# Reordering the column tiles of an input projection: attention-gate tiles between the GLU pairs, four V tiles around the LayerNorm

## What is computed

```python
p_x = h_x @ w_in[i]                      # 1024 x 8192
q_x = apply_rope(rms(p_x[..., Q0:K0]), cos, sin)
k_x = apply_rope(rms(p_x[..., K0:V0]), cos, sin)
v_x = p_x[..., V0:GA0]
att_x  = diff_attn_branch(q_x, k_all, v_all, ...)     # context and latent keys
a, g = jnp.split(p_x[..., U0:GC0], 2, axis=-1)
y = depthwise_conv(a * jax.nn.sigmoid(g), conv_w, conv_b)   # 31 taps
conv_x = silu(layernorm(y, ln_g, ln_b))               # over the 1024 channels
mixed_x = concatenate([att_x  * silu(p_x[..., GA0:U0]),
                       conv_x * silu(p_x[..., GC0:IN_W])])
y_x = mixed_x @ w_out[i]
```

## Time and profile before

| | |
|---|---|
| median of 3 runs | 2513.55 us (2512.09 to 2514.61) |
| span of the profiled execution, first to last instruction | 2509.4 us |
| own time of the profiled execution | not listed apart; the median is 4.15 us over its span |
| mean granted TensorE clock | 0.974 |
| PE busy | 2317.3 us, 92% of the span |
| DVE / POOL / ACT busy | 1323.7 / 875.1 / 849.3 us |
| taps of the convolution (L999) | 365.2 us, 240 instructions |
| ACT table loads | 9 of 1.28 us in the whole kernel |

### The profile page before, as it was taken

How to read it: one execution, slowest core, us unless ns; L and a number is a source line. 1 busy time by engine, 2 the same in 40 slices (tenths; PEclk the granted TensorE clock), 3 DMA queues, 4 the chain that set the end, 5 groups by cost and what they waited for, 6 DMA issues and landing times. The chain is left out here.

```text
span 2509.4 us, 30851 instructions
## 1 busy us (share of the span) xinstructions
PE 2317.3 (92%) x10898; PEld 1846.8 (74%) x10898; DVE 1323.7 (53%) x1373; ACT 849.3 (34%) x1244; POOL 875.1 (35%) x600
## 2 busy tenths in 40 slices
PE   4799999999968999999999999968888888899998
PEld 2445888888746788887787788857777777788787
DVE  5754339999992200016556540079999995800101
ACT  5745511111101212222222211157777774222221
POOL 0004823333311222221221222136656653844443
PEclk9999999999989999999999999989999997999999
DMA  8977621111111122221221232332221105153433
GB/s 290 337 247 219 193 66 46 50 46 46 46 42 51 55 72 71 67 72 54 72 75 53 72 97 72 87 89 57 59 59 48 48 1 206 67 176 127 160 129 108
DMA packets 227184, 246.46 MB, mean 98 GB/s; under 512 B 11277, under 2 KB 163853, under 8 KB 225583
## 3 DMA queue, kind: packets, MB, share of 16 engines
q1 hardware_dynamic: 225680, 235.11, 29.8%
q0 software_dynamic: 1440, 10.49, 1.1%
HBM read 214.09 MB, written 31.47 MB: 98 GB/s over the span
## 5 line engine op out<-in xcount | busy, mean ns | idle before, releaser
L448 POOL TENSOR_TENSOR w_lo<-w_raw,w_hi 128x512 fp32r<-128x512 f32 x288 | 402.7, 1409 | 1067.3 <-ACT w_hi L700 1066.9
L570 PE MATMUL psum<-h_hi,w_hi 128*128 128x512 f32 x1792 | 561.6, 395 | 6.5 <-POOL w_lo L448 4.9
L570 PE MATMUL psum<-h_hi,w_lo 128*128 128x512 f32 x1792 | 552.8, 390 | 0.0
L570 PE MATMUL psum<-h_lo,w_hi 128*128 128x512 f32 x1792 | 552.6, 390 | 0.0
L700 ACT ACTIVATE w_hi<-w_raw 128x512 fp32r<-128x512 f32 x288 | 180.8, 631 | 1036.9 <-PE psum L570 729.6
L570 PEld LDWEIGHTS psum<-h_hi,w_hi 128*128 128x128 f32 x1792 | 337.3, 188 | 85.3 <-issue 16.5
L570 PEld LDWEIGHTS psum<-h_lo,w_hi 128*128 128x128 f32 x1792 | 337.1, 188 | 70.6
L570 PEld LDWEIGHTS psum<-h_hi,w_lo 128*128 128x128 f32 x1792 | 336.9, 188 | 70.3
L999 DVE SCALAR_TENSOR_TENSOR conv<-y_pad,tap_w,conv 128x1024 f32<-128x1024 f32 x240 | 365.2, 1522 | 9.4
L1675 POOL TENSOR_TENSOR wo_lo<-wo_raw,wo_hi 128x512 fp32r<-128x512 f32 x128 | 175.8, 1380 | 188.4 <-ACT wo_hi L1758 188.4
L84 PE MATMUL psum<-wo_hi,m_hi 128*128 128x512 f32 x512 | 202.0, 395 | 10.7 <-DVE m_lo L1791 6.5
(11 more groups left out here) (174 smaller groups left out, 3182.8 us busy)
## 6 DMA issues: line engine op xcount, KB each, us to landing
w_raw<-in_w_in_dram SPq DMA_DIRECT2D x288, 256.0 KB, 3.0
ada_w<-in_w_ada_dram SPq DMA_DIRECT2D x32, 1024.0 KB, 6.8
wo_raw<-in_w_out_dram SPq DMA_DIRECT2D x128, 256.0 KB, 3.0
proj<-stage SPq DMA_DIRECT2D x40, 512.0 KB, 3.1
gate_w<-in_w_ada_dram SPq DMA_DIRECT2D x16, 1024.0 KB, 5.0
x_tok<-in_x_dram POOLq DMA_DIRECT2D x8, 1024.0 KB, 7.2
k_raw<-proj SPq DMA_DIRECT2D x16, 512.0 KB, 5.7
q_raw<-proj SPq DMA_DIRECT2D x16, 512.0 KB, 6.2
```

The costliest lines, as they stand in the source:

```text
L448: pool.tensor_tensor(w_lo[:, c], w_raw[:, c], w_hi[:, c].bitcast(F32), ALU.subtract).then_inc(w_lo_ready[c], 1)
L570: mm = pe.matmul(bank(2 * s_ + hf), w[:, c, j, :], x[:, jj, hf * BANK:(hf + 1) * BANK], start=(jj == 0 and w is w_hi and x is h_hi), stop= ...
```

## The change

The tiles of the projection are computed in another order. New numbers: U and GA in triples 16 to 39 (value, gate, GA tile), V 0 to 3 at 40 to 43, GC 44 to 51, K 52 to 59, Q 60 to 67, V 4 to 7 at 68 to 71. The rows of `proj` in DRAM stay where they were, now by `ROW_*` constants. PE takes the mean sums after V 0 and V 1, the sums of squares after V 2, then V 3. On ACT, two tiles (V 0, V 1) stand before the squares and V 2 right after them, with a load of the Sqrt table ahead of it; the split of V 3's weights is in `to_stage` of V 2. GA tiles take the parity of their number, so U tiles now use either pair of banks. Waits and counts of stores follow. Nothing is added to or left out of the computation.

```diff
@@ -50,7 +50,9 @@
 
 
 
-N_VC, N_KC, N_U, N_GA, N_GC, N_K, N_Q, N_V, N_END = 0, 8, 16, 32, 40, 48, 56, 64, 72
+N_VC, N_KC, N_U, N_V0, N_GC, N_K, N_Q, N_V4, N_END = 0, 8, 16, 40, 44, 52, 60, 68, 72
+
+ROW_GA, ROW_GC, ROW_K, ROW_Q, ROW_V, ROW_END = 0, 8, 16, 24, 32, 40
 
...
@@ -385,41 +387,70 @@
                 for s_ in range(2):
...
+            load_w(N_U, U0)
+            store_ctx(N_U - 3, 1, ctx_normed, CT - 2)
+            load_w(N_U + 1, U0 + CONV_W)
+            store_ctx(N_U - 2, 0, ctx_normed, CT - 1)
+            store_ctx(N_U - 1, 1, ctx_normed, CT)
+            load_w(N_U + 2, GA0)
+            load_w(N_U + 3, U0 + P)
+            load_w(N_U + 4, U0 + CONV_W + P)
+            store_after_act(N_U + 2, ROW_GA, 0)
+            load_w(N_U + 5, GA0 + P)
+
+            with sp.Fori(1, CT // 2) as i:
+                for s_ in range(2):
+                    n = N_U + 6 * i + 3 * s_
+                    load_w(n, U0 + (2 * i + s_) * P)
+                    load_w(n + 1, U0 + CONV_W + (2 * i + s_) * P)
+                    store_after_act(n - 1, ROW_GA + 2 * i + s_ - 1, 1 - s_)
+                    load_w(n + 2, GA0 + (2 * i + s_) * P)
+
+            load_w(N_V0, V0)
+            load_w(N_V0 + 1, V0 + P)
+            store_after_act(N_V0 - 1, ROW_GA + CT - 1, 1)
+            for k in range(2, 4):
+                load_w(N_V0 + k, V0 + k * P)
+                store_after_act(N_V0 + k - 2, ROW_V + k - 2, k % 2)
+            for k in range(2):
+                load_w(N_GC + k, GC0 + k * P)
+                store_after_act(N_GC + k - 2, ROW_V + k + 2, k)
+            with sp.Fori(1, CT // 2) as i:
+                for s_ in range(2):
+                    load_w(N_GC + 2 * i + s_, GC0 + (2 * i + s_) * P)
...
             for s_ in range(2):
-                load_w(N_U + s_, U0 + s_ * CONV_W)
-                store_ctx(N_U + s_ - 3, 1 - s_, ctx_normed, CT + s_ - 2)
-            store_ctx(N_U - 1, 1, ctx_normed, CT)
-            with sp.Fori(1, CT) as i:
-                for s_ in range(2):
-                    load_w(N_U + 2 * i + s_, U0 + i * P + s_ * CONV_W)
-            for n0, col0, last_store, own_store in ((N_GA, GA0, None, store_after_act),
-                                                    (N_GC, GC0, store_after_act, store_gc),
-                                                    (N_K, K0, store_gc, store_qk),
-                                                    (N_Q, Q0, store_qk, store_qk),
-                                                    (N_V, V0, store_qk, store_after_act)):
-                for s_ in range(2):
-                    load_w(n0 + s_, col0 + s_ * P)
-                    if last_store:
-                        last_store(n0 + s_ - 2, s_)
-                if n0 == N_K:
-
-                    sp.wait_ge(conv_used, CT)
-                    sp.dma_start(cos[:], t["rope_cos"]).then_inc(rope_landed, 16)
-                    sp.dma_start(sin[:], t["rope_sin"]).then_inc(rope_landed, 16)
+                load_w(N_K + s_, K0 + s_ * P)
+                store_gc(CT + s_ - 2, s_)
+
+            sp.wait_ge(conv_used, CT)
+            sp.dma_start(cos[:], t["rope_cos"]).then_inc(rope_landed, 16)
+            sp.dma_start(sin[:], t["rope_sin"]).then_inc(rope_landed, 16)
+            for n0, col0, k0 in ((N_K, K0, 0), (N_Q, Q0, CT)):
+                if k0:
+                    for s_ in range(2):
+                        load_w(n0 + s_, col0 + s_ * P)
+                        store_qk(k0 + s_ - 2, s_)
                 with sp.Fori(1, CT // 2) as i:
                     for s_ in range(2):
                         load_w(n0 + 2 * i + s_, col0 + (2 * i + s_) * P)
-                        own_store(n0 + 2 * i + s_ - 2, s_)
+                        store_qk(k0 + 2 * i + s_ - 2, s_)
+            for k in range(2):
+                load_w(N_V4 + k, V0 + (4 + k) * P)
+                store_qk(2 * CT + k - 2, k)
+            for k in range(2, 4):
+                load_w(N_V4 + k, V0 + (4 + k) * P)
+                store_after_act(N_V4 + k - 2, ROW_V + 4 + k - 2, k % 2)
...
@@ -583,9 +614,13 @@
                     pe.wait_ge(psum_freed, n + s_ - N_U - 1)
                     tile(n + s_, s_)
 
-            with pe.Fori(1, CT) as i:
-                pair(N_U + 2 * i)
-            pair(N_GA)
+            for n in range(N_U + 2, N_U + 6):
+                pe.wait_ge(psum_freed, n - N_U - 1)
+                tile(n, n % 2)
+            with pe.Fori(1, CT // 2) as i:
+                for q in range(3):
+                    pair(N_U + 6 * i + 2 * q)
+            pair(N_V0)
 
             pe.wait_ge(ctx_root, CT)
             for i in range(CT):
@@ -594,15 +629,16 @@
                     mm = pe.matmul(bank(4 + hf), mean_ones[:], conv[:, i, hf * BANK:(hf + 1) * BANK],
                                    start=(i == 0), stop=(i == CT - 1))
             mm.then_inc(mean_done, 1)
-            pair(N_GA + 2)
+            pe.wait_ge(psum_freed, N_V0 + 2 - N_U - 1)
+            tile(N_V0 + 2, 0)
             for i in range(CT):
                 pe.wait_ge(ln_squared, i + 1)
                 for hf in range(2):
                     mm = pe.matmul(bank(6 + hf), mean_ones[:], evac[:, i % 2, hf * BANK:(hf + 1) * BANK],
                                    start=(i == 0), stop=(i == CT - 1))
                 mm.then_inc(ln_sq_used, 1)
-            with pe.Fori(2, 4) as i:
-                pair(N_GA + 2 * i)
+            pe.wait_ge(psum_freed, N_V0 + 3 - N_U - 1)
+            tile(N_V0 + 3, 1)
             with pe.Fori(0, 4) as i:
                 pair(N_GC + 2 * i)
 
@@ -622,14 +658,13 @@
                     tile(n, s_)
                     pe.wait_ge(qk_root, 2 * i + s_ - 1)
                     qk_sums(2 * i + s_ - 1, (s_ + 1) % 2)
-            pe.wait_ge(psum_freed, N_V - N_U - 1)
-            tile(N_V, 0)
+            pe.wait_ge(psum_freed, N_V4 - N_U - 1)
+            tile(N_V4, 0)
             pe.wait_ge(qk_root, 2 * CT - 1)
             qk_sums(2 * CT - 1, 1)
-            pe.wait_ge(psum_freed, N_V - N_U)
-            tile(N_V + 1, 1)
-            with pe.Fori(1, 4) as i:
-                pair(N_V + 2 * i)
+            pe.wait_ge(psum_freed, N_V4 - N_U)
+            tile(N_V4 + 1, 1)
+            pair(N_V4 + 2)
 
         @block.scalar
...
@@ -751,18 +786,24 @@
                     ctx_square(k, s_)
                     ctx_sqrt(k - 1, (s_ + 1) % 2)
 
-            def glu_value(n, i, first=False):
+            def glu_value(n, i, s_):
                 split_w(n + 1)
                 act.wait_ge(tile_done, n + 1)
-                if not first:
-                    act.wait_ge(glu_used, i)
-                nc.scalar.activation(evac[:, 0, :], bank(0, 2), ACT.Copy).then_inc(psum_freed, 1)
-
-            def glu_gate(n):
+                act.wait_ge(glu_used, i)
+                nc.scalar.activation(evac[:, 0, :], bank(2 * s_, 2), ACT.Copy).then_inc(psum_freed, 1)
+
+            def glu_gate(n, s_):
...
@@ -770,33 +811,31 @@
             act.preload_act_table(ACT.Sigmoid)
             act.wait_ge(tile_done, N_U + 1)
             nc.scalar.activation(evac[:, 0, :], bank(0, 2), ACT.Copy).then_inc(psum_freed, 1)
-            glu_gate(N_U + 1)
-            with act.Fori(1, CT) as i:
-                glu_value(N_U + 2 * i, i)
-                glu_gate(N_U + 2 * i + 1)
-
-            def to_stage(n, s_, count, func, last=False):
-
-                if not last:
-                    split_w(n + 1)
-                act.wait_ge(tile_done, n + 1)
-                act.wait_ge(stored[s_], count)
-                nc.scalar.activation(stage[:, s_, :], bank(2 * s_, 2), func).then_inc(psum_freed, 1)
-
-            act.preload_act_table(ACT.Silu)
-            for k in range(4):
-                to_stage(N_GA + k, k % 2, 16 * (CT + k // 2), ACT.Silu)
+            glu_gate(N_U + 1, 1)
+            to_stage(N_U + 2, 0, 16 * CT, ACT.Silu)
+            glu_value(N_U + 3, 1, 1)
+            glu_gate(N_U + 4, 0)
+            to_stage(N_U + 5, 1, 16 * CT, ACT.Silu)
+            with act.Fori(1, CT // 2) as i:
+                for s_ in range(2):
+                    n = N_U + 6 * i + 3 * s_
+                    glu_value(n, 2 * i + s_, s_)
+                    glu_gate(n + 1, 1 - s_)
+                    to_stage(n + 2, s_, 16 * (CT + i), ACT.Silu)
+
+            for k in range(2):
+                to_stage(N_V0 + k, k, 16 * (CT + 4), ACT.Copy)
             for i in range(CT):
                 act.wait_ge(centred, i + 1)
                 if i >= 2:
                     act.wait_ge(ln_sq_used, i - 1)
                 nc.scalar.activation(evac[:, i % 2, :], conv[:, i, :], ACT.Square).then_inc(ln_squared, 1)
+            act.preload_act_table(ACT.Sqrt)
+            to_stage(N_V0 + 2, 0, 16 * (CT + 5), ACT.Copy)
             act.wait_ge(ln_sq_used, CT)
             nc.scalar.activation(evac[:, 0, :], bank(6, 2), ACT.Sqrt, bias=eps_col).then_inc(ln_root, 1)
             act.preload_act_table(ACT.Silu)
-            with act.Fori(2, 4) as i:
```

(62 more changed lines are left out.)

9 lines of the change are left out of this document (4 added, 5 removed).

## The result

The changed kernel takes 2469.28 us (median of 4 runs, 2467.24 to 2477.22) against 2514.08 us of the kernel before on the same chip. The ratio is 0.9831, with a 95% interval of 0.9815 to 0.9846: 1.7% faster, 44.8 us by the medians. The span of the profiled execution is 2465.6 us, 43.8 less than before. The forecast was 2470.6 us, 42.9 us less than before.

A forecast was written before the change was run, and what follows sets the result against it. PE, busy 92% of the span, was taken as the bound, so its idle or slow time counted. 41.90 + 2.62 - 1.6 = 42.9 us gained; 2513.55 - 42.9 = 2470.6 us, range 2467 to 2480.

The forecast's parts named there:

- What PE loses: PE's losses in the stage before the change, idle or slow, read from ACT's timeline: together 44.5 us.
- The mean, 34.03 us: At the mean's sums for the last convolution: PE loses 34.03 us, 31.9 of it idle, and the change gains it.
- Triples, 7.87 us: Tiles 18 to 33, before the mean: triples let DVE get ahead of ACT, so the 7.87 us lost there go.
- the squares, 2.62 us: At the squares' sums: taken after V 2, they start without waiting for the first square; 2.62 us gained.
- The last convolution: On DVE: done by 869.5 us, before the mean's sums begin at 882.1, with V 0 and V 1 as cover.
- V 3, 1.6 us lost: Ahead of V 3: its weight split now stands behind the squares and a table load, so PE loses 1.6 us.
- The tail: LayerNorm's tail: root done at 827.6, all at 844.4 on the old clock, hidden by V 3; cost nothing.
- Table loads, 18 us on ACT and none on PE: U stage: 14 more loads of 1.28 us on ACT fall in its idle time, 2.5 us remaining; PE never sees them.
- The loop of six tiles: PE's loop body grows from two tiles to six: taken as 0, from above 8 us.
- GC 0 or at a loop turn: Rival: some gain is given back at V 3, GC 0 or loop jumps, up to some 10 us: 2480; chance 0.10.
- Exposed table loads: Rival: each table switch on ACT stands in a split's way, 18 us go: 2489; chance 0.05.
- The slower rival: ACT is held in `glu_value` in every triple; six give back 47 us, all seven give 2525.7; chance 0.02.

## Why the prediction was right, step by step

- **What PE loses.** 44.5 us, read off from a ruler of chunks. The stage got 43.57 us shorter with one new wait of 1.16, which makes 44.7 us of losses removed. The kernel that splits V 3's weights earlier, with no wait left behind its first tile, is 44.98 us shorter in the stage than the kernel before.
- **The mean, 34.03 us.** Alone, in the old order, its removal gave 33.76, in which the clock took 1.70 us at the squares and gave 1.27 back behind the wait of 4.9 us; without these two it is 34.19.
- **Triples, 7.87 us, and the squares, 2.62 us.** They were not run apart. Together, less the 1.16 us of V 3, they should give 9.33 us; the difference between the changed kernel and the one with later sums is 9.81. The half microsecond between is the granted clock, which behind the same two waits cost that kernel something else than the kernel before: it loses 6.60 at GA 0 and 2.63 + 1.70 at the squares, and less the 1.16 that makes 9.77.
- **The last convolution.** Predicted to end by 869.5, it ended at 869.97; the sums were to begin at 882.1 and began at 881.52. Idle time of DVE per triple: about 15 predicted, 14.81 measured. A convolution takes 65.28 - 14.81 = 50.47 us and not 49.8: the 49.8 was a mean over eight, and the last of them ran with POOL idle (39.69 us for its taps). It changed nothing here, with a cover of 43.52 us.
- **V 3, 1.6 us lost.** Measured 1.16 of idle time, or 1.41 by the kernel that splits V 3's weights early, and the clock stayed at 1.00. That it would stay was argued from one row, and this was partly luck: in the old order with later sums it fell behind the same 2.63 us and took 1.70 more. What was off in the idle time is when PE would otherwise have started. I took the start of the next tile's first record, 823.36, which overlaps the sums. From the end of the sums, 809.93 + 14.00 = 823.93, the same working gives 824.97 - 823.93 = 1.04.
- **The tail.** The root was put 2.6 us after V 3's start, the end of the LayerNorm 2.3 us ahead of V 3's end. Measured: 934.07 against 932.09, and 952.07 against about 953.9. It is hidden by that little, and by the 5.4 us more of which the prediction spoke. ACT's sum of 827.6 is 827.5 when redone, which changes nothing.
- **Table loads, 18 us on ACT and none on PE.** ACT's busy time rose by 19.6 us. The step was right, but its slack was put too small: 2.5 us are what is left before a split is *late*, and 17.5 are left before PE feels it.
- **The loop of six tiles.** Taken at nothing; PE shows no wait at its turns.
- **The rivals.** No wait came at GC 0 or at a loop turn. Exposed table loads are refuted by the kernel with 18 more. The slower rival, ACT held in every triple, is a real mechanism: it came with twenty more taps, at the idle time per hold that was given. But it held only four times there, and the wait of 66.84 us at the mean's sums, which that rival left out, cost more than the 32.4 us of all holds. The change is clear of it, by 14.81 us a triple; with eight more taps it was 2.6.
- **The time.** 2470.6 forecast, 2469.28 measured; 42.9 us of gain against 43.57 in the stage and 44.8 by the medians. That the two times agree to 1.3 us is in part chance, for the four runs spread over 10 us; the agreement that counts is that of the stage. The lower bound, 2470.6 - 1.6 less 1.3, is 2467.7 and not 2467.5.

## What to carry to other kernels

Where one engine's work per step is longer than another's, look at the lag that adds up and at the first place that must wait for *all* of it: here the reduction over eight convolutions cost 34.0 us, and the lag on the way there 7.9. Work that does not depend on the slow engine is worth most between its last step and that reduction: two tiles there, in the old order, gave 33.76 of 43.57 us. What one part of such a change is worth depends on the other: with the triples in place the same two tiles are worth 18.19. And read a queue's slack to the engine that needs its result (17.5 us), not to the next entry of the queue (2.5 us).

## What the runs showed of the hardware that was not expected

- The part ahead of the stage varies by up to 8.45 us between profiles of identical code there: the first GLU value is evacuated at 341.95, 342.94, 344.91, 343.70, 350.40, 345.85 and 346.92 us in the seven profiles with the new order. In the changed kernel's first 100 us the transfer engines are busy for 0.86, at 308 GB/s. The last three of the seven ran on another chip than the three before them; what sets the difference was not tried. A microsecond won later in the kernel shows in a ruler of its own stage and not in the span.
- A tap of 128x1024 on DVE depends on POOL: 30 of them take 48.27 us beside POOL's splits, 43.49 when PE's stall stops POOL for part of the time, and 39.69 when POOL is idle nearly throughout. Tap by tap the trace of the kernel before leaves no doubt that it is POOL: the 133 taps that no POOL instruction overlaps take 1.283 to 1.287 us, whether PE and ACT are busy or not, and the other 107 take 1.82 on average and up to 2.40. The Trainium skill ("GPSIMD Engine Reference", 1. Specifications) says that the two share their SBUF interfaces and contend where a DVE instruction has two SBUF inputs, as these have; the rows agree.
- The same wait does not always move the granted clock. Behind 1.16 us, and before behind 2.64, it stayed at 1.00; in the old order with later sums, behind 2.63 us at the same place, it was 0.50 from 822 to 825 us. Before, the 4.9 us brought it to 0.93 over 51 us. Behind the 15.07 us four records of the sums took 3.78 us, where four of the changed kernel's take 13.89 x 4 / 32 = 1.74. What decides between the two cases of 2.6 us stays open.
